# Gated delta rule in a two-block kernel: one decay product instead of two, key and score transposes in another place, and a small subtraction moved to GpSimd

## What is computed

```python
qkv = silu(causal_depthwise_conv(qkv, conv_b_w))      # q, k, v: (B, S, 8, 128)
q, k = l2_normalize(q), l2_normalize(k)
beta = sigmoid(beta_raw)                              # beta_raw, a_raw: the last 16 columns of x @ w_in
g = -exp(a_log) * softplus(a_raw + dt_bias)
...
gc = cumsum(g)                                        # inside a chunk
decay = exp(where(incl, gc[i] - gc[j], -inf))
kb = k * beta
low = where(strict, einsum(kb, k) * decay, 0)
rhs = concat([v * beta, kb * exp(gc)])
sol = triangular_solve(low + eye, rhs)                # -> u, w
attn = einsum(q, k) * decay
q_dec = q * exp(gc)
k_dec = k * exp(g_last - gc)
# chunk by chunk
v_new = u_i - w_i @ state
o_i = q_i @ state + attn_i @ v_new
state = state * exp(g_last) + k_i.T @ v_new
o = rms_norm(o, gdn_norm_g) * silu(z_b)
```

## Time and profile before

| | us |
|---|---|
| median of 3 runs | 901.56 (901.53 to 902.18) |
| the profiled execution, its own time | 902.52 |
| span from its first to its last instruction | 900.7 |
| TensorE busy in the span | 884.0 |
| GpSimd / ScalarE / VectorE busy | 668.7 / 504.7 / 459.7 |

### The profile page before, as it was taken

How to read it: one execution, slowest core, us unless ns; L and a number is a source line. 1 busy time by engine, 2 the same in 40 slices (tenths; PEclk the granted TensorE clock), 3 DMA queues, 4 the chain that set the end, 5 groups by cost and what they waited for, 6 DMA issues and landing times.

```text
span 900.7 us, 18968 instructions
## 1 busy us (share of the span) xinstructions
PE 884.0 (98%) x7503; PEld 816.7 (91%) x7503; DVE 459.7 (51%) x979; ACT 504.7 (56%) x712; POOL 668.7 (74%) x480
## 2 busy tenths in 40 slices
PE   6999999999999999999999999999999999999997
PEld 6999999999997889999999999888997899998886
DVE  4368763485532633777768776635666442220004
ACT  5775533763336456565677656556576356664331
POOL 5986766457656888958776786769796579989882
PEclk9999999999999999999999999999999999999999
DMA  8664544435444565645444555455552357666631
GB/s 317 209 225 126 162 133 128 129 107 164 142 128 168 183 188 174 202 124 171 151 132 129 164 158 150 145 192 187 158 198 91 94 161 226 203 198 208 197 118 47
DMA packets 40824, 146.08 MB, mean 162 GB/s; under 512 B 4512, under 2 KB 4640, under 8 KB 40736
## 3 DMA queue, kind: packets, MB, share of 16 engines
q1 hardware_dynamic: 39296, 140.71, 49.5%
q10 hardware_dynamic: 1440, 4.16, 1.3%
HBM read 143.81 MB, written 1.05 MB: 161 GB/s over the span
## 4 chain that ended last, share of the span: by engine, by line
PE 90%; DVE 3%; ACT 2%; issue 2%; POOL 2%; DMA 1%; SPq 0%; DVEq 0%; ACTq 0%; POOLq 0%
PE dense L509 25%; PE dense L510 24%; PE dense L511 24%; PE bank L870 2%; POOL wlo L484 1%; PE dense L565 1%; PE bank L707 1%; POOL wlo L483 1%; PE bank L708 1%; DVE cv L1716 1%; DMA raw<-weight_units_dram 1%; PE bank L902 1%; PE bank L856 1%; ACT whi L1130 1%; PE bank L1013 1%
## 5 line engine op out<-in xcount | busy, mean ns | idle before, releaser
L484 POOL TENSOR_TENSOR wlo<-raw,whi 128x512 fp32r<-128x512 f32 (+1 forms) x259 | 409.3, 1587 | 22.7 <-ACT whi L1130 22.6
L1130 ACT ACTIVATE whi<-raw 128x1024 fp32r<-128x1024 f32 (+1 forms) x262 | 273.3, 1057 | 231.7 <-PE dense L511 198.1
L483 POOL TENSOR_TENSOR wlo<-raw,whi 128x512 fp32r<-128x512 f32 x195 | 253.7, 1301 | 179.2 <-ACT whi L1130 177.2
L509 PE MATMUL dense<-x_hi,whi 128*128 128x256 f32 x1232 | 350.3, 284 | 6.9 <-DVE wlo L1647 6.5
L510 PE MATMUL dense<-x_lo,whi 128*128 128x256 f32 x1232 | 343.0, 278 | 0.0
L511 PE MATMUL dense<-x_hi,wlo 128*128 128x256 f32 x1232 | 342.8, 278 | 0.0
L509 PEld LDWEIGHTS dense<-x_hi,whi 128*128 128x128 f32 x1232 | 232.7, 189 | 10.9 <-DVE x_lo L1636 6.5
L510 PEld LDWEIGHTS dense<-x_lo,whi 128*128 128x128 f32 x1232 | 232.9, 189 | 0.7 <-issue 0.2
L511 PEld LDWEIGHTS dense<-x_hi,wlo 128*128 128x128 f32 x1232 | 233.0, 189 | 0.0
L509 PE MATMUL dense<-whi,ya_hi 128*128 128x512 f32 x192 | 77.4, 403 | 1.0 <-issue 0.8
L511 PE MATMUL dense<-whi,ya_lo 128*128 128x512 f32 x192 | 75.0, 391 | 0.0
(11 more groups left out here) (336 smaller groups left out, 1374.5 us busy)
## 6 DMA issues: line engine op xcount, KB each, us to landing
raw<-weight_units_dram SPq DMA_DIRECT2D x261, 512.0 KB, 3.9
xtok<-in_x_dram SPq DMA_DIRECT2D x1, 1024.0 KB, 7.7
gb<-in_ln_g_dram ACTq DMA_DIRECT2D x2, 512.0 KB, 4.5
gb<-in_ln_b_dram ACTq DMA_DIRECT2D x2, 512.0 KB, 6.4
out_dram<-zt SPq DMA_DIRECT2D x3, 256.0 KB, 2.0
qT<-x_turned_dram SPq DMA_DIRECT2D x2, 256.0 KB, 4.4
raw<-weight_units_dram SPq DMA_DIRECT2D x2, 256.0 KB, 4.6
qT<-x_turned_dram SPq DMA_DIRECT2D x1, 512.0 KB, 7.1
```

Source lines behind the costliest of these rows:

```text
L483: pool.tensor_tensor(wlo[:, slot, 0:half], unit_slot(u)[:, 0:half], whi[:, slot, 0:half].bitcast(F32), ALU.subtract)
L484: pool.tensor_tensor(wlo[:, slot, first:2 * half], unit_slot(u)[:, first:2 * half], whi[:, slot, first:2 * half].bitcast(F32), ALU.subtrac ...
L509: pe.matmul(out_, lh, rh, start=start, stop=False, skip_group_check=True)
L1130: act.activation(whi[:, u % NSPL, first:], unit_slot(u)[:, first:], ACT.Copy).then_inc(hi_done, 1)
```

## The change

- Stage 0 makes one matrix of gate sums (`B`) and no longer `A`. ScalarE writes its exp to `AT`, once for each g, in place of two exps.
- Stage 1 makes the scores as queries x keys, so that `B` has the queries on the partitions. VectorE makes `EL` head by head, with beta over the squared norm as a scalar for each partition, and multiplies both score matrices into `AT` only after that, behind both `EL`. It signals this on the new semaphore `gdn_scored`.
- Stage 2 waits for `gdn_scored` before it overwrites `B` of g = 1. Stage 3 turns `AT` in the place of the keys, and VectorE masks the result.
- The keys are turned ahead: `key_transposes`, 8 transposes behind the units 14 and 41, into the A banks. ScalarE squares the result (`key_squares`), VectorE sums it along the rows (`key_sums`), and stage 0 of VectorE multiplies the turned keys into `KX`. `k_sums_of` goes, with the square in ScalarE's `conv_gate` and `take_k_sums`.
- The sums of the gates are copied by VectorE in step 15 (`gate_taken`), and ScalarE takes their exp in place. Stage 0 of TensorE waits for the copy, not for the exp.
- The gate factors are made in two operations instead of three, with the sign of `EL` in beta (-0.5 instead of 0.5). Two copies in the stages 16 and 18 become a multiplication by -1.
- `blank` (the unit matrices in `XN`) stands one or two steps later on ScalarE; one pair of table loads between half 0 and half 1 goes.
- The subtraction for `tail_lo` moves from VectorE's step 7 to GpSimd, behind the low part of unit 12.

The diff, cut to its core:

```diff
+KEYS_BEHIND = (14, 41)
@@ gpsimd, in the loop over u, behind the low part of unit u
+                if u == 12:
+                    pool.wait_ge(tail_split, 1)
+                    pool.tensor_tensor(tail_lo[:, :, :], tail_w[:, :, :], tail_hi[:, :, :].bitcast(F32), ALU.subtract).then_inc(tail_low, 1)
@@ tensor
-            def k_sums_of(p):
-                ...
-                pe.wait_ge(k_squares, p + 1)
-                bank = pair_of("gd_kq", p)[0]
-                for i in range(2):
-                    for t in range(NT):
-                        last = pe.matmul(bank[:, 2 * i + t:2 * i + t + 1], cv[:, 0, i * T + t * P:i * T + (t + 1) * P], ones[:, 0:1],
-                                         start=True, stop=True)
-                last.then_inc(k_sums, 1)
+            def key_transposes(half):
+                if half == 0:
+                    pe.wait_ge(rest_loaded, 16)
+                else:
+                    pe.wait_ge(gdn_vector, dve_step(0, 19, 1))
+                    pe.wait_ge(gdn_squares, 2)
+                pe.wait_ge(conv_silu, 3 * (2 * half + 1) + 1)
+                for g in range(2):
+                    for u in range(4):
+                        last = pe.transpose(SB[2 * g][:, u * P:(u + 1) * P], kT[:, 4 * half + u, g * P:(g + 1) * P], ident)
+                    last.then_inc(k_turned, 1)
@@ tensor, gdn
                         if half == 0:
-                            pe.wait_ge(gate_exp, 1)
+                            pe.wait_ge(gate_taken, 1)
                     elif s == 1:
                         ...
                         pe.wait_ge(gdn_vector, dve_step(half, 0, g))
+                        pe.wait_ge(gdn_exp, 3 * half + g + 1)
                         if s == 0:
-                            pe.matmul(A[:, o], upto, unit(GAF[:, g, :], u), start=True, stop=True)
-                            last = pe.matmul(B[:, o], unit(GAF[:, g, :], u), upto, start=True, stop=True)
+                            last = pe.matmul(B[:, o], upto, unit(GAF[:, g, :], u), start=True, stop=True)
                         elif s == 1:
-                            last = pe.matmul(B[:, o], kT[:, h, tok], qT[:, h, tok], start=True, stop=True)
+                            last = pe.matmul(B[:, o], qT[:, h, tok], kT[:, h, tok], start=True, stop=True)
                         elif s == 2:
                             last = pe.transpose(A[:, o], unit(EL[:, g, :], u), ident)
                             if g == 1:
+                                if u == 0:
+                                    pe.wait_ge(gdn_scored, 2 * half + 2)
                         elif s == 3:
-                            pe.transpose(A[:, o], kT[:, h, tok], ident)
+                            pe.transpose(A[:, o], unit(AT[:, g, :], u), ident)
@@ scalar
-                if part == "k":
-                    act.activation(cv[:, 0, :].rearrange("p (h t) -> p h t", h=2), dst, ACT.Square).then_inc(k_squares, 1)
+            def key_squares(half):
+                for g in range(2):
+                    act.wait_ge(k_turned, 2 * half + g + 1)
+                    act.activation(LT[:, g, :], SB[2 * g][:, :], ACT.Square).then_inc(k_squares, 1)
                     if s == 0:
-                        link(act.activation(A[:, :], A[:, :], ACT.Exp))
-                        act.activation(B[:, :], B[:, :], ACT.Exp).then_inc(gdn_exp, 1)
+                        act.activation(AT[:, g, :], B[:, :], ACT.Exp).then_inc(gdn_exp, 1)
-                    if s in (2, 20):
+                    if s == 2 or (half, s) == (1, 20):
                         tables(SILU_TABLES)
@@ vector
+            def key_sums(half):
+                for g in range(2):
+                    vec.wait_ge(k_squares, 2 * half + g + 1)
+                    link(vec.tensor_reduce(kn[:, 0, g, 4 * half:4 * half + 4], four(LT[:, g, :]), AX_X, ALU.add), k_taken)
                     if s == 0:
-                        link(vec.tensor_tensor(four(EL[:, g, :]), four(A[:, :]), heads(g, 8, half), ALU.mult))
-                        vec.tensor_tensor(four(AT[:, g, :]), four(B[:, :]), all4(upto), ALU.mult).then_inc(gdn_vector, 1)
+                        vec.tensor_tensor(four(KX[:, g, :]), four(A[:, :]), heads(g, 6 + g, half), ALU.mult).then_inc(gdn_vector, 1)
                     elif s == 1:
-                        link(vec.scalar_tensor_tensor(EL[:, g, :], A[:, :], -1.0, EL[:, g, :], ALU.mult, ALU.mult))
-                        vec.tensor_tensor(AT[:, g, :], B[:, :], AT[:, g, :], ALU.mult).then_inc(gdn_vector, 1)
+                        for u in range(4):
+                            cols, h = slice(u * P, (u + 1) * P), 4 * half + u
+                            link(vec.scalar_tensor_tensor(EL[:, g, cols], A[:, cols], gt[:, 4, g, h:h + 1], AT[:, g, cols], ALU.mult, ALU.mult),
+                                 gdn_vector if u == 3 else vec_chain)
+                        if g == 1:
+                            for i in range(2):
+                                link(vec.tensor_tensor(AT[:, i, :], SB[2 * i + 1][:, :], AT[:, i, :], ALU.mult), gdn_scored)
-                if n == 7:
-                    vec.wait_ge(tail_split, 1)
-                    vec.tensor_tensor(tail_lo[:, :, :], tail_w[:, :, :], tail_hi[:, :, :].bitcast(F32), ALU.subtract).then_inc(tail_low, 1)
...
```

More of the change, by code:

```diff
@@ L329, in build @@
         gdn_exp = sem("gdn_exp")
+        gdn_scored = sem("gdn_scored")
         gdn_squares = sem("gdn_squares")
@@ L735, in gdn @@
                         pe.wait_ge(gdn_vector, dve_step(half, 0, g))
+                        pe.wait_ge(gdn_exp, 3 * half + g + 1)
                     elif s == 3:
                         pe.wait_ge(conv_silu, 3 * (2 * half + 2))
+                        pe.wait_ge(gdn_scored, 2 * half + g + 1)
                         pe.wait_ge(gdn_vector, dve_step(half, 2, g))
@@ L820, in _ @@
                     gate_sums_of()
-                if n < FIRST_YA and n % 8 == 5:
-                    k_sums_of(n // 8)
+                if n in KEYS_BEHIND:
+                    key_transposes(KEYS_BEHIND.index(n))
                 if n in GDN_AT:
@@ L1331, in _ @@
                     gdn(1, 0)
+                if n in KEYS_BEHIND:
+                    key_squares(KEYS_BEHIND.index(n))
+                if n - 1 in GDN_FIRST:
+                    blank(GDN_FIRST.index(n - 1))
                 for j in range(KT):
@@ L1345, in _ @@
                     if n + 1 == GDN_FIRST[0]:
-                        act.wait_ge(gate_sums, 1)
-                        act.activation(gt[:, 6, :, :], SB[3][:, 0:2 * GH].rearrange("p (t h) -> p t h", t=2), ACT.Exp).then_inc(gate_exp, 1)
-                        settle(gate_exp)
+                        act.wait_ge(gate_taken, 1)
+                        link(act.activation(gt[:, 6, :, :], gt[:, 6, :, :], ACT.Exp))
                     key_norms(GDN_FIRST.index(n + 1))
-                    blank(GDN_FIRST.index(n + 1))
                     if n + 1 == GDN_FIRST[1]:
@@ L1666, in gates @@
                 vec.wait_ge(gates_tanh, 1)
-                link(vec.tensor_scalar(gt[:, 2, :, :], gt[:, 2, :, :], 1.0, 0.5, ALU.add, ALU.mult))
+                link(vec.tensor_scalar(gt[:, 2, :, :], gt[:, 2, :, :], 1.0, -0.5, ALU.add, ALU.mult))
                 vec.wait_ge(gates_log, 1)
@@ L1717, in conv @@
                          conv_done if back == 3 else vec_chain)
-            def take_k_sums(p):
-                vec.wait_ge(k_sums, p + 1)
-                link(vec.tensor_copy(kn[:, 0, :, 2 * p:2 * p + 2].rearrange("p t h -> p h t"),
-                    pair_of("gd_kq", p)[0][:, 0:4].rearrange("p (h t) -> p h t", h=2)), k_taken)
-                free("gd_kq", p)
+            def key_sums(half):
+                for g in range(2):
+                    vec.wait_ge(k_squares, 2 * half + g + 1)
+                    link(vec.tensor_reduce(kn[:, 0, g, 4 * half:4 * half + 4], four(LT[:, g, :]), AX_X, ALU.add), k_taken)
             def gate_factors(half):
@@ L1751, in gdn @@
                         vec.wait_ge(gdn_level, 2 * half + g + 1)
+                    elif s == 0:
+                        vec.wait_ge(k_turned, 2 * half + g + 1)
                     else:
@@ L1777, in gdn @@
                     elif s == 3:
-                        link(vec.tensor_tensor(four(KX[:, g, :]), four(A[:, :]), heads(g, 6 + g, half), ALU.mult))
+                        link(vec.tensor_tensor(four(AT[:, g, :]), four(A[:, :]), all4(upto), ALU.mult))
                         vec.tensor_tensor(four(VB[:, g, :]), four(B[:, :]), heads(g, 3, half), ALU.mult).then_inc(gdn_vector, 1)
@@ L1868, in _ @@
                     vec.wait_ge(consts_loaded, 16)
-                if n == 7:
-                    vec.wait_ge(tail_split, 1)
-                    vec.tensor_tensor(tail_lo[:, :, :], tail_w[:, :, :], tail_hi[:, :, :].bitcast(F32), ALU.subtract).then_inc(tail_low, 1)
-                    settle(tail_low)
                 if n == 14:
@@ L1883, in _ @@
                     r = n - 8 * p
```

(9 more changed lines are left out.)

23 lines of the change are left out of this document (9 added, 14 removed).

## The result

The changed kernel takes 908.40 us (median of 6 runs, 907.66 to 909.35), the kernel before beside it 902.35 us (6 runs): 1.007 times as long, interval 1.006 to 1.008. Slower was forecast, by 3.4 us. It is slower by 6.1, and 908.4 lies above the range of 902.6 to 907.2.

The account below looks back on a forecast made before the run. TensorE, busy 884.0 of 900.7 us, was taken as the bound. Terms of -5.2 us and +8.6 us for the tail's wait and clock gave +3.4, so 905.0 us, eight in ten within 902.6 to 907.2.

Parts of the forecast that it names:

- The tail: Behind unit 8, TensorE waits for GpSimd's `tail_lo`, made behind unit 12: 6.3 us added (6.0 to 6.9).
- Nothing gives this back: The tail's 6.3 us wait is never recovered, since all later work of TensorE is in its own queue.
- The clock: After the tail's wait, TensorE's clock falls and its return costs 2.3 us, bounds 0 and 3.0.
- Rival A: The tail's wait comes but the clock stays up, so its return costs nothing: 902.7 us, chance 0.12.
- Key sums: Four places, behind units 5, 13, 21 and 29, lose their small matmuls on TensorE: 3.4 us saved.
- decay product: Stage 0 loses half its 16 matmuls in both halves, and a wait for ScalarE's exp shortens: 3.9 us saved together.
- the transposes: Keys turned ahead at units 14 and 41, 16 transposes more on TensorE: 1.8 us added.
- ScalarE's order: Key squares in step 41 delay unit 44's bank some 3 us; costed at 0, or 0 to 2 us without cover.
- half 0 at nothing: In half 0 VectorE's stage 1 and 2 work ends before TensorE comes, so no wait is added.
- stages 1 and 2 of half 1: TensorE's waits for VectorE's `EL` and score products become 1.8 instead of 0.5 + 1.0: 0.3 us added.
- Rival C: A second new wait, from `EL` or unit 44's bank, or a long clock return: 907 to 908 us, chance 0.12.
- `EL` at its dear end: In stages 1 and 2 of half 1, VectorE's `EL` operations cost 0.482 each, adding 1.1 us beyond the forecast.

Follow-up runs that it names:

- e2: The changed kernel with the `tail_lo` subtraction on GpSimd behind unit 9 instead of unit 12: 900.50 us, 0.9978 of the kernel before.
- e3: The kernel before with one edit, the `tail_lo` subtraction on GpSimd behind unit 12: 909.15 us, 1.0076 of the kernel before.
- e4: The changed kernel with 44 matmuls that nothing reads in front of the tail's wait: 906.23 us, 1.0038 of the kernel before.
- e11: The same kernel as e1 run again, `tail_lo` subtraction back on VectorE's step 7: 909.34 us (898.82 to 911.12).
- e5: As e2, with one 512-column product for `EL` instead of four, leaving out beta and the key norm: 896.22 us.
- e8: As e2, with stage 1's two score products in the other order and ScalarE copying the turned scores, VectorE masking them later: 896.90 us.
- e1: The changed kernel with the `tail_lo` subtraction back on VectorE's step 7: 901.96 us, seven runs at 898.6 to 902.1, five at 907.9 to 911.1.
- e9: As e8, with the key transposes behind unit 14 in front of the gate sums instead of behind them: 896.99 us.

## Why the prediction was right in kind and too low

**Right.** *The tail.* It is the term that turns a gain into a loss; e2 and e3 show it from both sides. The wait was forecast at 6.3 and is 6.12, the subtraction at 0.35 and is 0.41 (0.37 to the next start). Both engines came 0.7 us earlier than I had them, which cancels; that the wait came out so near is in part luck. "Nothing gives this back" was too strong: e3 gives back 0.6 by unit 18, and in e2, without the tail's wait, TensorE waits 0.7 for the gates at L696 that the changed kernel does not. *The clock.* Forecast 2.3, bounds 0 to 3.0. The 20 steps from 40.01 to 44.23 take 4.22 us where 20 of 0.113 take 2.27, 1.9 more in the trace, and e4 gives 2.0 to 2.2. Rival A, the clock stays up, is out. The step by which I judged it, that the clock falls when matmuls have been absent for longer than the 4.9 us at the end, was loose: here it was down some 3.5 us after the last matmul. The Trainium skill ("TensorE: Matmul & The Clock Gate", Part 1) has idleness bring back the throttled level; the first fall agrees, TensorE having been idle from 33.9 on. The second is not told by idleness alone: e2 and e11 have the same two waits and a granted clock of 1.00. *Key sums, decay product:* -3.3 for -3.4 and -3.9 for -3.9; the transposes +1.4 for +1.8. *ScalarE's order* cost nothing: unit 44 finds its bank.

**Wrong, first: half 0 at nothing.** The prediction's step was: "In half 0 the same sum ends before TensorE comes, since nothing of the other mixer stands before it." That is so for stage 2, and I looked no further. VectorE has two operations more for each g, and in half 0 it goes without a gap from 79.64 to 99 us: stages 1, 2 and 3 and the convolution of the next projection follow each other. What is late at stage 1 is late at stage 4:

```profile
91.92 3.07 DVE L1728 SCALAR_TENSOR_TENSOR cv<-dense,columns,cv 128x255 f32<-128x255 f32 x6
95.14 0.69 DVE L1793 TENSOR_TENSOR AT<-bank,con 128x512 f32<-128x512 f32 x1
...
97.31 0.69 DVE L1794 TENSOR_TENSOR VB<-bank,gt 128x512 f32<-128x512 f32 x1
```

```profile
98.06 0.44 PE L722 MATMUL bank<-con,XN 128*128 128x128 f32 x2 [0.82 <-DVE VB L1794]
...
102.99 0.24 PE L714 MATMUL bank<-EL,XN 64*64 64x32 f32 x1 [0.43 <-DVE XN L1814]
```

TensorE loses 1.8 us from unit 23 to 27. Shortening `EL` (e5) takes the wait for `VB` away, and so does taking the scores' copy off VectorE (e8, where the shift from unit 23 to 27 is 1.4 us smaller than in e2): it is VectorE's load, not a bank or a semaphore.

**Wrong, second: stages 1 and 2 of half 1, +0.3 forecast, +2.1 measured.** `EL` was sized right: eight in 3.06 us, 0.38 from start to start, by the forecast 1.5 for each g. VectorE came to it some 0.4 us later than I had it, and the two waits are 0.9 + 1.1 = 2.0 against 1.8. That makes 0.3 of the 1.8. The other 1.5 is the clock's second fall, which is in no term: I had weighed the clock for a wait of 6 us alone. e2, with the same waits and no fall, has +1.33 between the units 46 and 48 where the changed kernel has +2.81. That the clock makes the difference is shown; what makes it fall here is not.

Both misses go the same way: 1.8 + 1.8 over, 0.5 under at the tail, 0.4 at the transposes, and 0.4 of an early start. Rival C came nearest (907 to 908), but of its three parts (`EL` at its dear end, unit 44 behind its bank, a long return of the clock) none came; what came is a second new wait in a place that it doesn't name.

**What the rest is worth.** Without the tail's wait the change is faster: 1.8 us (e2), against 5.2 forecast for the same parts. The 3.4 between are half 0 (1.8), the waits of half 1 (0.3), the wait for `gt` at L696 (0.7), and 0.6 that fits the second fall in five of e2's eleven executions: the six without it have a median of 899.8, 2.5 us under the kernel before.

**Open.** Why the tail on VectorE's step 7 (e1, e11) gives two groups 9 us apart, when the tail on GpSimd behind unit 9 does not: no trace of a slow one exists. A guess is that `tail_lo` or another result comes now before and now behind a point of TensorE's, so that a long wait comes and goes; no trace shows it. The clock alone is not enough: at the same mean granted clock of 0.996 one execution of this kernel takes 901.58 us and another 908.00. The slowest, 910.3 to 911.1, lie at 0.990 to 0.992, so the clock falls further in them as well. Open too is what makes the clock fall, or not, in stage 2 of half 1, and why e9's median does not show what its trace gains.

## What to carry to other kernels

When work is added to an engine that is not the bottleneck, follow it to the next place where that engine has a gap: up to there each later hand-over is late by the same amount, not only the first. When a small result moves to an engine's queue, count what stands before it there: the place in the queue (behind unit 12, where TensorE had to wait) cost 6.8 us alone (e3), the operation itself takes 0.4. And a wait of TensorE costs its length and perhaps the clock: 6.1 us idle cost 2 us more, and two waits of 1 us among transposes cost 1.5 more in some executions.

## What the hardware showed that was not expected

The granted clock fell in a stage where TensorE was idle for no longer than 1.12 us at once (0.59 over 194 to 196 us of the changed kernel, 0.60 over 188 to 190 in e1) and stayed at 1.00 in e2 with the same two waits. The kernel of e1 did both: in its second trace (e11) the clock stayed at 1.00. What tells these apart is open; all four run the same transposes between the waits. The clock's return took about 4 us of matmuls after the tail and, by the steps of unit 47, about 3 after the second fall.
